# A conditioning product moved from the mixing stage into the first stage, the recurrence and the output projection

## The reference

```python
silu_c = jax.nn.silu(c)
mod = silu_c @ w_ada[l] + b_ada[l]            # 2048 x 12288
sh1, sc1, g1, sh2, sc2, g2 = jnp.split(mod[:, None, :], N_ADA, axis=-1)
u = _modulate(_rms_norm(x, norm1_g[l]), sh1, sc1)
mix, _, _ = _mixer(u, ...)                    # ends with merged @ w_out
x = x + g1 * mix
x = x + g2 * _swiglu(_modulate(_rms_norm(x, norm2_g[l]), sh2, sc2), w_ffn_in[l], w_ffn_out[l])
return _rms_norm(x, norm_f_g)
```

## Time and profile before

| | us |
|---|---|
| median of three runs | 2695.63 |
| lowest, highest | 2693.99, 2695.93 |
| the profiled execution's own time | 2696.47 |
| its span in the trace | 2694.7 |
| PE busy | 2660.4 |
| DVE busy | 1585.1 |
| ACT busy | 1016.1 |

### The profile page before, as it was taken

One profiled execution on the slowest core, in us unless ns is written; L12 is line 12 of the kernel. 1 busy time (PEld: TensorE's weight loads), 2 busy tenths in 40 slices (PEclk: granted clock), 3 DMA queues, 4 the chain that ended last, 5 costly groups with the idle time before them and its releaser, 6 DMA issues.

```text
span 2694.7 us, 35961 instructions
## 1 busy us (share of the span) xinstructions
PE 2660.4 (99%) x13497; PEld 2223.4 (83%) x13497; DVE 1585.1 (59%) x1740; ACT 1016.1 (38%) x1138; POOL 69.8 (3%) x84
## 2 busy tenths in 40 slices
PE   7999999999999999999999999999999999999998
PEld 5788778888888888888788888888888888888887
DVE  5525878654555544633568878878787763343443
ACT  4214675222222222322335444444444442242333
POOL 0000000000000000000001000001010000000000
PEclk8999999999999999999999999999999999999999
DMA  9922223565556665644368888878888844544555
GB/s 366 362 72 86 90 86 105 189 202 187 191 189 195 196 194 177 189 145 140 102 178 202 211 196 203 202 200 201 199 202 196 211 138 156 182 157 163 184 175 192
DMA packets 443200, 485.88 MB, mean 180 GB/s; under 512 B 14904, under 2 KB 388992, under 8 KB 438016
## 3 DMA queue, kind: packets, MB, share of 16 engines
q1 hardware_dynamic: 411504, 371.57, 44.0%
q0 software_dynamic: 11520, 41.95, 8.8%
q10 hardware_dynamic: 20112, 71.48, 8.5%
HBM read 418.88 MB, written 24.12 MB: 164 GB/s over the span
## 4 chain that ended last, share of the span: by engine, by line
PE 97%; DMA 1%; DVE 1%; ACT 1%; ACTq 0%; issue 0%; SPq 0%; DVEq 0%
PE main L1033 15%; PE main L1034 15%; PE main L1035 15%; PE main L1361 10%; PE aux L1361 10%; PE main L1365 5%; PE aux L1365 5%; PE aux L1410 4%; PE aux L1411 4%; PE aux L1412 4%; PE main L1410 1%; PE main L1411 1%; PE main L1412 1%; PE aux L1199 1%; PE aux L1085 1%; DMA ada_pc<-in_w_ada 1%
## 5 line engine op out<-in xcount | busy, mean ns | idle before, releaser
L1033 PE MATMUL main<-u_both,w_hi 128*128 128x512 f32 x1536 | 611.1, 398 | 2.5 <-DVE u_both L1886 2.5
L1034 PE MATMUL main<-u_both,w_hi 128*128 128x512 f32 x1536 | 599.8, 390 | 0.0
L1035 PE MATMUL main<-u_both,w_lo 128*128 128x512 f32 x1536 | 598.7, 390 | 0.0
L1527 DVE TENSOR_TENSOR w_lo<-w_raw,w_hi 128x1024 fp32r<-128x1024 f32 x216 | 263.0, 1223 | 448.8 <-ACT w_hi L607 448.2
L607 ACT ACTIVATE w_hi<-w_raw 128x1024 fp32r<-128x1024 f32 x216 | 227.5, 1056 | 508.4 <-DMA w_raw<-in_w_in 314.1
L1033 PEld LDWEIGHTS main<-u_both,w_hi 128*128 128x128 f32 x1536 | 289.3, 188 | 75.3 <-issue 19.3
L1035 PEld LDWEIGHTS main<-u_both,w_lo 128*128 128x128 f32 x1536 | 289.1, 188 | 61.5
L1034 PEld LDWEIGHTS main<-u_both,w_hi 128*128 128x128 f32 x1536 | 289.3, 188 | 58.0 <-issue 4.1
L879 ACT ACTIVATE h_S<-f_S 128x1024 fp32r<-128x1024 f32 x160 | 165.3, 1057 | 228.7 <-DVE f_S L1929 95.4
L2032 DVE TENSOR_TENSOR hb_l<-hb_f,hb_h 128x2048 fp32r<-128x2048 f32 x33 | 75.7, 2292 | 256.6 <-ACT hb_h L941 256.6
L1410 PE MATMUL aux<-hb_h,bw_h 128*128 128x512 f32 x512 | 200.0, 391 | 0.9 <-DVE bw_l L2037 0.9
(11 more groups left out here) (274 smaller groups left out, 3966.4 us busy)
## 6 DMA issues: line engine op xcount, KB each, us to landing
w_raw<-in_w_in SPq DMA_DIRECT2D x144, 512.0 KB, 3.6
ada_pc<-in_w_ada ACTq DMA_DIRECT2D x128, 512.0 KB, 4.3
f_A<-in_w_ffn_in SPq DMA_DIRECT2D x120, 512.0 KB, 5.3
bw_f<-in_w_ffn_out SPq DMA_DIRECT2D x88, 512.0 KB, 6.8
f_S<-in_w_ffn_in SPq DMA_DIRECT2D x80, 512.0 KB, 4.2
f_S<-f_A POOLq DMA_DIRECT2D x80, 512.0 KB, 5.7
hb_f<-hidden_feature_major SPq DMA_DIRECT2D x33, 1024.0 KB, 4.9
ada_pc<-in_w_ada SPq DMA_DIRECT2D x48, 512.0 KB, 7.3
```

What stands on the lines that cost most here:

```text
L1033: pe.matmul(dst, wh, m_hi_ap, start=start, stop=False, skip_group_check=shared)
L1034: pe.matmul(dst, wh, m_lo_ap, start=False, stop=False, skip_group_check=shared)
L1035: return pe.matmul(dst, wl, m_hi_ap, start=False, stop=stop, skip_group_check=shared)
L1527: dve.tensor_tensor(w_lo[:, s], w_raw[:, s], w_hi[:, s].bitcast(F32), ALU.subtract).then_inc(lo_done, 1)
```

## The change

The eight parts of the conditioning product leave the mixing stage. Parts 0 to 2 go to the first stage, with SP as the issuer of the chunks; part 3 goes to the recurrence, two chunks a window, issued by ACT; parts 4 to 7 go to the output projection, one an iteration, issued by ACT and distributed over its steps by the table `OUT_CHUNKS`. The first four parts use `ada2_pc`, now in another region, the last four `ada2_pw`; each has two buffers of one chunk, as before. PE's sums (now the function `spread`) stand after the half steps of tiles 14 and 15, in the middle of unit 12, ahead of the recurrence, in the first mixing iteration, after the first unit of output iterations 1 to 3, and after the first units of SwiGLU. `mod2` is written in four pieces (`mod2_out`) instead of one, and some buffers change their place.

```diff
+OUT_CHUNKS = {1: (0, 1), 2: (2, 3, 4), 3: (5, 6), 4: (7, 8, 9), 5: (10, 11, 12), 6: (13, 14, 15)}
...
-        ada2_pc = sb("ada2_pc", "ada", [2, 1024])
+        ada2_pc = sb("ada2_pc", "pf", [2, 1024])
+        ada2_pw = sb("ada2_pw", "lru", [2, 1024])
...
+            def ada2(*chunks):
+
+                for n in chunks:
+                    i, cc, q = n // 16, n % 16, n % 2
+                    if n > 1:
+                        sp.wait_ge(ada2_used[q], n // 2)
+                    src = ada_t[:, cc, 2 * D + 1024 * i:2 * D + 1024 * i + 1024]
+                    sp.dma_start(ada2_pc[:, q, :], src).then_inc(ada2_landed[q], 16)
+
             sp.wait_ge(raw_out, 16)
             sp.dma_start(x_fm, x_raw[:, :, :]).then_inc(x_stored, 16)
-            for u in range(8, 16):
+            sp.wait_ge(root_done, 6)
+            ada2(*range(4))
+            xa_unit(8)
+            xa_unit(9)
+            ada2(*range(4, 16))
+            xa_unit(10)
+            xa_unit(11)
+            for u in range(12, 16):
+                ada2(*range(4 * u - 32, 4 * u - 28))
                 xa_unit(u)
...
                 for u in range(4):
+                    if first:
+                        ada2(*range(32 + 4 * u, 36 + 4 * u))
                     unit(base, per, i, u0 + u, in_t[:, UC * u:UC * u + UC, ds(h * UN + I_YA, UN)])
...
             def window(h, hh, p, base, per, i, u0, first=False):
                 for u in range(4):
                     hi(base, per, i, u0 + u + 2)
+                    if u == 0:
+                        for q in range(2):
+                            act.wait_ge(ada2_used[q], h + 24)
+                            src = ada_t[:, ds(h * 2 + q, 1), 2 * D + 3072:2 * D + 4096]
+                            act.dma_start(ada2_pc[:, q, :], src.rearrange("p o n -> p (o n)")).then_inc(ada2_landed[q], 16)
...
-            def ada2(i, cc):
-                q = cc % 2
-                act.wait_ge(ada2_used[q], i * 8 + cc // 2)
-                act.dma_start(ada2_pc[:, q, :], ada_t[:, cc, ds(i * 1024 + 2 * D, 1024)]).then_inc(ada2_landed[q], 16)
...
-                    if u == 0:
-                        ada2(i, 0)
-                    if u < 15:
-                        ada2(i, u + 1)
...
                         for k in range(14, KT):
                             mixed_hi(k)
+                        act.wait_ge(unit_used, G_OUT)
+                    for cc in OUT_CHUNKS.get(u, ()):
+                        q = cc % 2
+                        act.wait_ge(ada2_used[q], i * 8 + (32 + cc // 2))
+                        act.dma_start(ada2_pw[:, q, :], ada_t[:, cc, ds(i * 1024 + (2 * D + 4096), 1024)]).then_inc(ada2_landed[q], 16)
                     if u == 3 or (u == 7 and not last):
...
+            def spread(i):
+
+                pe.wait_ge(ada2_used[1], i * 8 + 8)
+                for t in range(8):
+                    ins = pe.matmul(aux[:, 2, ds(i * 8 + t, 1)], ada2_acc[:, t * P:t * P + P], ones[:, 0:1], start=True, stop=True)
+                ins.then_inc(acc_used, 1)
...
                 for k in (14, 15):
                     xa_half(k, j)
+            spread(0)
...
+                        if u == 12 and n == 0:
+                            spread(1)
...
+            spread(2)
             window(0, 0, 0, G_YX, 4, 0, 0)
...
+                            if first and j == 0 and k == 0:
+                                pe.wait_ge(tanh_done, 16)
+                                spread(3)
...
-                pe.wait_ge(ada2_used[1], i * 8 + 8)
-                for t in range(8):
-                    ins = pe.matmul(aux[:, 0, ds(i * 8 + t, 1)], ada2_acc[:, t * P:t * P + P], ones[:, 0:1], start=True, stop=True)
-                ins.then_inc(acc_used, 1)
-
...
                         unit(G_OUT, 8, i, 4 * j + k, j, u_of(k), k == 0, k == 3, half_done if last and j and k == 3 else None)
-
-            with pe.Fori(0, 3) as i:
+                        if not first and j == 0 and k == 0:
+                            spread(i + 3)
...
             up_first()
+            spread(7)
...
+            def ada2(buf, i, cc, k, first):
+
+                q = cc % 2
+                dve.wait_ge(ada2_landed[q], i * 128 + 16 * (cc // 2 + 1))
+                if first:
+                    dve.wait_ge(acc_used, i)
+                    ins = dve.tensor_scalar(ada2_acc[:, :], buf[:, q, :], cvec[:, k, 0:1], None, ALU.mult)
+                else:
+                    dve.wait_ge(ada2_used[1 - q], i * 8 + (cc + 1) // 2)
+                    ins = dve.scalar_tensor_tensor(ada2_acc[:, :], buf[:, q, :], cvec[:, k, 0:1], ada2_acc[:, :], ALU.mult, ALU.add)
+                ins.then_inc(ada2_used[q], 1)
...
+                if r == 3:
+                    ada2_early(*range(4))
...
             lo(0, 8, 0, 8)
             lo(0, 8, 0, 9)
+            ada2_early(*range(4, 16))
             xa_out(0, 0)
             xa_out(0, 1)
             for u in range(8, 16):
                 lo(0, 8, 0, u + 2)
+                ada2_early(*range(4 * u - 16, 4 * u - 12))
                 if u % 4 == 3:
...
-                    if first and u == 1:
+                    if last and u == 1:
                         second_modulation()
...
                         residual(i * 4 + (2 * j + 1), 2 * j + 1, j, 1).then_inc(pair_free[j], 1)
+                    for cc in OUT_CHUNKS.get(u, ()):
+                        ada2(ada2_pw, i + 4, cc, cc, cc == 0)
```

More of the change, by code:

```diff
@@ L797, in _ @@
             chunk_out(2)
-            ada2(0, 2)
             hi(G_MIX, 16, 0, 7)
             chunk_out(3)
-            for u in (3, 4, 5):
-                ada2(0, u)
             for g in range(4):
@@ L1285, in _, with out_proj @@
                 mix(i)
-            def out_proj(i, last=False):
+            def out_proj(i, first=False, last=False):
                 for j in range(2):
```

64 lines of the change are left out of this document (34 added, 30 removed).

## The result

The changed kernel takes 2806.65 us (median of 4 runs, 2802.9 to 2810.58) beside 2694.81 us for the kernel before (4 runs, 2693.97 to 2695.93): 4.15% slower, ratio 1.0415 with a 95% interval of 1.0397 to 1.0433, or 111.8 us. Predicted were 2768.5 us and a range of 2735 to 2800. The direction, the stages and the longest wait came as forecast; the sum was 39 us short, and the time lies 6.65 us above the range, so the forecast failed in size. The profiled execution took 2810.58 us, with a span of 2808.8.

A forecast was written before the change was run, and what follows sets the result against it. PE was taken to bound the kernel, busy throughout all touched stages. First stage 39.6 us plus output projection 33.2 made 72.8 on the profiled 2696.5, 2769.3, less 0.8 to the median: 2768.5 us, range 2735 to 2800.

The forecast's parts named there:

- wait 1: First stage: PE wants tile 14 at 143.2 us but it is ready at 146.7; 3.5 us.
- wait 2: First stage: PE's first sum waits from 155.1 to 178.2 us for chunk 15's product; 23.1 us.
- wait 3: First stage, middle of unit 12: the second sum waits for chunk 31, used at 221.7 us; 2.3 us.
- wait 4: End of the first stage: the third sum waits for chunks 32 to 47, done at 261.8 us; 9.0 us.
- recurrence, mixing: Recurrence: two chunks a window stay hidden by DVE's 3.52 us wait for ACT; mixing gains nothing; 0 us each.
- waits of the output projection: Output projection: late w_lo and sums cost 6.6 us, then 6.5 in iterations 1 and 2, 2.1 in the last.
- wait of the norm: After the output projection: the last residual stands behind chunk 15 and a w_lo, so the norm's chain waits 11.5 us.
- Nothing gained by the removal: Mixing stage: PE is busy throughout and its eight sums return elsewhere, so taking chunks off DVE and ACT gains 0.
- The round trip of two buffers sets the pace: Issue, landing, product, next issue: 5.0 us in the first stage, 5.2 in the output projection, for two chunks.
- Landings of 3.6 and 3.8: A chunk's DMA was taken to land in 3.6 us in the first stage, 3.8 in the output projection.
- the rival with landings of 4.3: Landings as long as in mixing: first stage pays 54 us, output projection 47, time 2796; chance 0.20.
- The clock, counted once: First stage, after the wait for the first sum: PE's clock is lower for 3.5 us, costing 1.7 us, counted once.

The follow-up runs named there:

- the hold run: Kernel before, with PE held seven times in mixing iterations 1 to 7 for one 8 KB transfer each; 2721.43 us, ratio 1.0096.

## Where the prediction was right, and where it failed

The sum was 72.8 us and 111.8 were measured. The mechanism held, and the term that failed is the clock: counted once with 1.7 us, it cost 30. The table has the gaps between starts of PE's matmuls in the profiled execution, less the usual 0.2 us, and the clock by the pairing. That execution lies 114.1 us above the profiled one of the kernel before, 2 more than the medians.

| term | predicted | measured |
|---|---|---|
| wait 1, tile 14 | 3.5 | 4.4 |
| wait 2, first sum | 23.1 | 22.9 |
| wait 3, second sum | 2.3 | 8.8 |
| wait 4, third sum | 9.0 | 10.8 |
| clock, first stage | 1.7 | 13.6 (8.4, and 5.2 in three sums) |
| recurrence, mixing | 0 | 0 |
| waits of the output projection | 21.7 | 26.4 |
| wait of the norm | 11.5 | 10.8 |
| clock, output projection | 0 | 16.8 (15.1, and 1.7 in one sum) |

- *Nothing gained by the removal:* right. Mixing got shorter by its sums alone, to 0.15 us an iteration, and the recurrence hid its chunks: from the first gates to Fourier it is 228.30 us, where it was 226.45, and 1.7 of that is the sum that moved there.
- *The round trip of two buffers sets the pace:* right as a mechanism. More buffers took 82 of the 112 us away. That wait 2 was met within 0.2 us is in part luck: chunk 15 was used at 180.6 where I had 178.1, since a trip took some 5.4 us and not 5.0, and PE came to the sum at 157.8 where I had 155.1, since wait 1 was longer and half-speed matmuls stood behind it. The two errors cancel.
- *Landings of 3.6 and 3.8:* too short. They were 4.3 in the median for SP's chunks and 4.9 for ACT's, by the rows of lines 396 and 838; the rival with landings of 4.3 (2796) was nearer in the total, but not for its reason: it has 101 us of waits, the forecast 71, and 84 were measured.

```profile
DMA to landing us min/median/max: 3.3/4.3/17.9
```

```profile
DMA to landing us min/median/max: 3.4/4.9/8.3
```

  The output projection's waits nevertheless came out only 4 us above the forecast (37 against 33.2). By the sensitivity given, 2.8 us for each 0.1, landings of 4.9 should have added 31. Why they didn't is not shown. Two things may hide a part, by my inference: ACT's lead over DVE, and that PE, 17 us slower in this stage by the clock, wants each `w_lo` later.
- *Places in the output projection:* right in part. I had the last unit of an iteration 2.2 us late and the first of the next 3.4 late, each time alike. Measured were 5.4 before the last unit of the first iteration and none behind it, then 0.7 and 4.4, then 5.3 and 1.0, and 4.2 before the last unit of all. The sums between the iterations waited 3.1, 0.7 and 1.6, where I had 1.1 each.
- *Wait 3:* 2.3 us forecast, 8.8 measured. The trips behind unit 12 were longer, as DVE's timeline shows:

```profile
200.96 2.67 DVE L1572 SCALAR_TENSOR_TENSOR ada_acc<-ada_pc,cvec,ada_acc 128x1024 f32<-128x1024 f32 x2 [7.54 <-DMA ada_pc<-in_w_ada]
...
231.63 1.28 DVE L1572 SCALAR_TENSOR_TENSOR ada_acc<-ada_pc,cvec,ada_acc 128x1024 f32<-128x1024 f32 x1 [1.64 <-DMA ada_pc<-in_w_ada]
```

  SP issued unit 12 at 194.90, where I had 190.0, since the first sum began 2.5 us later and it and the start of unit 8 ran at half clock. That delay came to PE as well, which reached the second sum's place at 224.2 in place of 219.4. What made the wait longer is the rest: from the issue to the end of chunk 31 it was 232.9 - 194.9 = 38.0 us in place of 31.7; six trips took 6.3 us each with the splits between them, which I had left out of the count.
- *The clock, counted once:* this is the step that failed. I took 1.7 us behind one wait, for the whole change. There are 14 waits of 0.7 us and more between starts, and besides them PE lost 30.4 us at the lower clock, 28.7 more than I had. Waits above 3 us cost 1.6 to 3.9 us each in this way, sums included; the three of 0.7 to 0.9 us cost 0.1 to 0.2, and the one of 1.6 cost 1.9. Without this miss the forecast would have stayed inside its range: the waits alone were 13 us longer than I had (84 against 71). Half-speed windows, the runs with PE held, and the slow starts that go where PE is kept at work say that it is the clock; how much each of them gives back differs (12 us by the medians, 16 by the pairing).
- *Two slips of arithmetic:* 5.44 is 174.2 / 32, not 175 / 32, and by the two sensitivities landings of 4.0 give 2782, not 2779. Neither matters for the outcome.

The Trainium skill, page "TensorE: Matmul & The Clock Gate", section "HAM oscillation — how this bites in real kernels", tells that waits for DMA between bursts of matmuls put the clock down anew each time, so that the penalty is paid by the wait and not once. The rows agree in kind, and I did not weigh this rule in the prediction. In size they differ: that page's case gives 26.7 us for 32 waits, by my estimate 0.83 each, and here a wait of 4.7 us costs 2.2 beyond its length.

The rule to double-buffer (the Trainium skill, page "Trainium Kernel Development and Optimization", section "Best Practices") was rightly set aside: two buffers in turn cost 44 us in the output projection that four took back.

## What to carry to other kernels

Work that is free beside a saturated engine isn't free elsewhere, though that stage shows idle time on the engine that gets it: ask how many of its transfers may be in flight at once, and compare a round trip divided by the buffers with the time between uses. Where a stage needs several chunks per step, give it at least as many buffers as a step has chunks (here four did for three chunks; three buffers were not tried), and keep them out of the instruction order ahead of whatever the bounding engine wants next. When you price a stall of PE, add to each wait of 3 us and more about 2 us of half-speed matmuls, once for every wait; the waits of 0.7 to 0.9 us cost next to nothing beyond their length here.

## What the hardware did that I had not expected

- The cost of a wait of PE beyond its length hardly grows with it: 0.8 us on average for one of 2.7, 2.2 for 4.7, 2.3 for 8.7. In the changed kernel the one wait of 23 us cost 3.9 (a slow sum and slow matmuls), and the seven of 2.7 in the hold run 6 together, in waits of 19 us.
- A landing is no property of the transfer. The same 512 KB took 3.9 us at 197 GB/s with two buffers, 4.6 at 231 GB/s when the products were thin, and 9.1 at 382 GB/s with eight buffers. Shorter work between transfers alone bought 1.5 us of the first sum's wait of 23, more transfers in flight 12.
